# First norm of a streaming encoder step: rows turned and scaled in one product with a diagonal matrix of the roots, instead of scaled in place and then transposed

## What is computed

```
def _rmsnorm(x, g):
    y = xf * lax.rsqrt(jnp.mean(xf * xf, axis=-1, keepdims=True) + EPS)
    return y * g
...
h = _rmsnorm(x, g_mix[l])
qa, ka, va, qb, kb, vb, rb, a1, ga, gb = split(h @ w_in)
```

## Time and profile before

| what | value |
|---|---|
| median of three runs | 950.14 us |
| the profiled execution | 951.9 us |
| its span | 950.2 us |
| TensorE matmul busy | 897.2 us, 94% |
| VectorE busy | 577.5 us, 61% |
| ScalarE busy | 421.0 us, 44% |
| GpSimd busy | 273.9 us, 29% |

### The profile page before, as it was taken

The page is one execution under the profiler, slowest core; times in us unless marked ns, Lnnn a source line. Parts: engine busy times, 40 slices in busy tenths (PEclk is TensorE's granted clock), DMA queues, the critical chain, the costliest instruction groups (busy, mean ns, idle before and its releaser), DMA issues.

```text
span 950.2 us, 17215 instructions
## 1 busy us (share of the span) xinstructions
PE 897.2 (94%) x7051; PEld 855.9 (90%) x7051; DVE 577.5 (61%) x1115; ACT 421.0 (44%) x751; POOL 273.9 (29%) x161
## 2 busy tenths in 40 slices
PE   3999999999889999999999968899999999999997
PEld 3889999989888889888999958899999999999997
DVE  5582656557784445565545667785259884278842
ACT  5552443534453544445444445563235662155432
POOL 2442313222323223232333102225322225222351
PEclk9999999999998999999999979999999999999999
DMA  8323122121421221212114427774357774277522
GB/s 239 89 72 85 57 77 68 56 73 50 110 67 52 61 68 46 67 46 68 46 35 141 109 64 164 165 164 123 111 107 172 175 169 133 58 166 156 138 72 64
DMA packets 154293, 94.59 MB, mean 100 GB/s; under 512 B 4064, under 2 KB 145078, under 8 KB 154214
## 3 DMA queue, kind: packets, MB, share of 16 engines
q1 hardware_dynamic: 138246, 71.88, 26.9%
q0 software_dynamic: 9504, 17.31, 10.6%
q10 hardware_dynamic: 6464, 4.29, 1.7%
HBM read 71.87 MB, written 3.60 MB: 79 GB/s over the span
## 4 chain that ended last, share of the span: by engine, by line
PE 68%; DVE 15%; ACT 6%; DMA 6%; issue 3%; ACTq 1%; SPq 0%; POOL 0%; DVEq 0%; POOLq 0%
PE G L583 13%; PE G L585 12%; PE G L584 12%; PE X L845 3%; PE X L847 3%; PE X L848 3%; PE G L845 3%; PE G L847 3%; PE G L848 3%; DMA wraw<-in_w_up_dram 3%; PE X L752 2%; DVE qAT L1542 2%; DMA csum<-csum 2%; PE X L736 2%; PE X L723 1%
## 5 line engine op out<-in xcount | busy, mean ns | idle before, releaser
L583 PE MATMUL G<-h_hi,w_hi 128*128 128x272 f32 x1296 | 389.2, 300 | 6.7 <-DVE rv L1505 2.8
L585 PE MATMUL G<-h_hi,w_lo 128*128 128x272 f32 x1296 | 375.9, 290 | 0.0
L584 PE MATMUL G<-h_lo,w_hi 128*128 128x272 f32 x1296 | 374.6, 289 | 0.0
L532 POOL TENSOR_TENSOR w_lo<-wraw,w_hi 128x1024 fp32r<-128x1024 f32 x85 | 215.7, 2541 | 423.9 <-ACT w_hi L946 423.9
L583 PEld LDWEIGHTS G<-h_hi,w_hi 128*128 128x128 f32 x1296 | 245.3, 189 | 18.4 <-issue 13.8
L584 PEld LDWEIGHTS G<-h_lo,w_hi 128*128 128x128 f32 x1296 | 245.7, 190 | 0.6
L585 PEld LDWEIGHTS G<-h_hi,w_lo 128*128 128x128 f32 x1296 | 245.2, 189 | 0.0
L946 ACT ACTIVATE w_hi<-wraw 128x1024 fp32r<-128x1024 f32 x129 | 135.1, 1050 | 64.3 <-PE G L585 38.6
L1840 DVE TENSOR_TENSOR rs<-G,rv 128x544 f32<-128x544 f32 x24 | 17.4, 724 | 79.5 <-PE G L585 79.5
L1146 ACT ACTIVATE prob<-prob,nm 128x256 f32<-128x256 f32 (+2 forms) x80 | 36.7, 460 | 63.0 <-DVE sd L1574 63.0
L540 POOL DMA_DIRECT2D wraw<-csum x22 | 18.8, 857 | 158.6 <-DVE csum L1721 102.0
(11 more groups left out here) (299 smaller groups left out, 1826.4 us busy)
## 6 DMA issues: line engine op xcount, KB each, us to landing
wraw<-in_w_in_dram SPq DMA_DIRECT2D x53, 512.0 KB
wraw<-in_w_gate_dram SPq DMA_DIRECT2D x22, 512.0 KB
wraw<-in_w_up_dram SPq DMA_DIRECT2D x22, 512.0 KB
csum<-csum POOLq DMA_DIRECT2D x44, 256.0 KB, 6.2
wraw<-in_w_down_dram SPq DMA_DIRECT2D x16, 512.0 KB
wraw<-csum POOLq DMA_DIRECT2D x22, 256.0 KB, 3.5
wraw<-in_w_out_dram SPq DMA_DIRECT2D x8, 512.0 KB
wraw<-in_w_down_dram SPq DMA_DIRECT2D x8, 384.0 KB
```

The lines of the kernel that those rows point to most:

```text
L532: pool.tensor_tensor(w_lo[:, slot, :, :], wraw[:, slot, :, :], w_hi[:, slot, :, :].bitcast(F32), ALU.subtract).then_inc(w_split, 1)
L583: pe.matmul(o, w_hi[:, slot, kc, :], b_hi[:, kc, cols], start=(kc == 0), stop=False)
L584: pe.matmul(o, w_hi[:, slot, kc, :], b_lo[:, kc, cols], start=False, stop=False)
L585: mm = pe.matmul(o, w_lo[:, slot, kc, :], b_hi[:, kc, cols], start=False, stop=(kc == last))
```

## The change

The in-place scaling on ScalarE and VectorE goes. VectorE writes five diagonal matrices `root_diag` (in the memory of `att`) with the roots of the frames on the diagonal, and the turn of a row block is an ordinary float32 product of the block with its diagonal matrix, in place of a transposition with the identity.

```
-SCALE_ACT, SCALE_DVE = (0, 2), (1, 3, 4)
...
+        root_diag = att
...
             def turn_input(c):
-                if c % (KC // 2) == 0:
-                    pe.wait_ge(x_scaled_act, len(SCALE_ACT) * (1 + c // (KC // 2)))
-                    pe.wait_ge(x_scaled_dve, len(SCALE_DVE) * (1 + c // (KC // 2)))
                 if c >= 3:
                     pe.wait_ge(h_ok, c - 2)
                 for j, (t0, nt) in enumerate(TOK):
-                    mm = pe.transpose(TURNED[c % 3][:, t0:t0 + nt], xtok[0:nt, j, c * P:(c + 1) * P],
-                                      ident[0:nt, 0:nt])
+                    if c == 0:
+                        pe.wait_ge(diag_ok, j + 1)
+                    mm = pe.matmul(TURNED[c % 3][:, t0:t0 + nt], xtok[0:nt, j, c * P:(c + 1) * P],
+                                   root_diag[0:nt, j, 0:nt], start=True, stop=True)
                 mm.then_inc(x_turned, 1)
...
             high_part(0)
-            act.wait_ge(x_root, 1)
-            for part in range(2):
-                for j in SCALE_ACT:
-                    x = xtok[0:TOK[j][1], j, part * D // 2:(part + 1) * D // 2]
-                    act.activation(x, x, ACT.Copy, scale=rt[0:TOK[j][1], j:j + 1])\
-                        .then_inc(x_scaled_act, 1)
             act.wait_ge(param_ok, 1)
...
             refine(rv[:, 0:NJ], rt[:, 0:NJ], rs[:, 0:NJ], x_root)
+            dve.wait_ge(x_root, 1)
+            dve.wait_ge(const_pool, 1)
+            for j, (t0, nt) in enumerate(TOK):
+                dve.tensor_scalar(root_diag[0:nt, j, 0:nt], ident[0:nt, 0:nt], rt[0:nt, j:j + 1], None, ALU.mult)\
+                    .then_inc(diag_ok, 1)
             dve.wait_ge(setup_pe, 1)
             dve.tensor_copy(param[:, :], G[0][:, 0:24]).then_inc(param_ok, 1)
-            dve.wait_ge(x_root, 1)
-            for part in range(2):
-                for j in SCALE_DVE:
-                    x = xtok[0:TOK[j][1], j, part * D // 2:(part + 1) * D // 2]
-                    dve.tensor_scalar(x, x, rt[0:TOK[j][1], j:j + 1], None, ALU.mult).then_inc(x_scaled_dve, 1)
-
             dve.wait_ge(param_ok, 1)
```

More of the change, by code:

```diff
@@ L344, in mixer_program @@
         x_root = sem("x_root")
-        x_scaled_act = sem("x_scaled_act")
-        x_scaled_dve = sem("x_scaled_dve")
+        diag_ok = sem("diag_ok")
         x_turned = sem("x_turned")
```

## The result

The changed kernel takes 960.31 us (median of 4 runs, 957.77 to 960.95) against 949.55 before. The ratio is 1.0098, 95% interval [1.0063, 1.0132]: slower by 6 to 13 us, about 1%. The profiled execution took 960.69 us, its span 958.9.

What follows compares the result with a forecast made beforehand. TensorE, busy 94% of the span, was taken as the bound. An earlier start against slower turns summed to −0.3 to +0.4 us, put as no change, 950.2 us; range 947.1 to 954.2.

Steps and rivals of the forecast that it cites:

- What costs nothing: Work beside the turns: ScalarE, parameter copy and scalings, w_lo, DMA and VectorE were claimed to add no time.
- the 3.5 that I had named as a sign of being wrong: Weight tile 0: the prediction is wrong if chunk 7 starts more than 3.5 us away from 31.15.
- something unpriced further on: Later stretches of slow clock and of waits could fall otherwise; chance 0.05, split evenly between slower and faster.
- The product's price: Turns: a float32 product takes two passes, five passes more per turn, 0.55 us fast or 1.10 slow.
- The rival with four passes: Turns: a product costs four times a transposition's 0.11 us, giving +8.6 us, 958.8 us; chance 0.03.
- The fifth diagonal held: At the start, the sample tile's diagonal waits behind GpSimd's w_lo until 15.33 us, stalling turn 0.
- case B: At the start, the fifth diagonal is held until 15.33; turn 7 ends at 29.8 us, +0.4 us.
- The clock: TensorE at the start: rise to 2.4 GHz 5.2 us after the first ordinary product, near 17.5 us.
- late clock and case B: Start: clock rises at 24.5 and the fifth diagonal is held, +3.5 us, 953.7; late clock's chance 0.25.
- A shift is handed on one to one: Behind the first product TensorE has no gap, so a shift at 31 us reaches the total about one to one.
- The middle of A and B as forecast: Midpoint of fifth diagonal unheld (−0.3 us) and held (+0.4 us): no change, 950.2 us.
- the earlier start: TensorE's first turn starts at 12.33 instead of 15.45 us, 3.12 us earlier, since diagonals replace the scaling.

Runs made afterwards that it cites:

- e9: Kernel before, with 39 small idle transpositions (78 TensorE instructions) added at the start: 954.20 us, ratio 1.0054.
- e8: Kernel before, with GpSimd's first w_lo waiting for VectorE's six scalings: 946.37 us, ratio 0.9960.
- e12: Kernel before, with GpSimd's wait for the scalings and 39 small idle transpositions (78 instructions): 951.52 us, ratio 1.0017.
- e1: The changed kernel run again, unedited: 959.16 us against 949.06 for the kernel before, ratio 1.0102.
- e7: The changed kernel with 88 small idle transpositions added at the start, 254 instructions more than the kernel before: 954.24 us, ratio 1.0039 to that kernel.
- e2: The changed kernel with GpSimd's first w_lo waiting for the five diagonals: 957.32 us, ratio 1.0087 to the kernel before.
- e11: The changed kernel with GpSimd waiting for the diagonals and 89 small idle transpositions, 256 instructions more than the kernel before: 949.76 us, ratio 1.0001.
- e3: The changed kernel with turns as identity transpositions, diagonals still made, scaling left out of the computation: 948.92 us, ratio 0.9995 to the kernel before.
- e6: Kernel before, with GpSimd waiting for the scalings and making w_lo of weight tile 0 three times; TensorE's program untouched: 953.00 us, ratio 1.0035.
- e10: Kernel before, with 128 small idle transpositions (256 TensorE instructions) added at the start: 948.59 us, ratio 1.0003.

## Why the prediction was wrong

The step that failed is "What costs nothing", with its sentence that no DMA is moved or added: it put the stretch behind the start at nothing. TensorE's own program is fetched by DMA, and the change makes it 78 instructions longer at the front; that moved its blocks onto other weight loads 550 us later, and loads that a block falls on took up to 9.7 us instead of 5.9 to 6.8. It cost 4.7 us alone (e9) and 5.4 us on e8's version (e12), and 5.6 and 8.1 us came back where it was taken away (e1 to e7, e2 to e11). In five traces with 78 more the stretch is 362.4 to 365.9 us, in two with 50 more 362.3 and 364.0, in seven with −2, 0, 254 or 256 it is 356.8 to 360.9. The start missed too: chunk 7 came 3.7 us late, beyond the 3.5 that I had named as a sign of being wrong, by the clock and the held diagonals below. I had put 0.05 on "something unpriced further on" and hadn't looked for it.

- **The product's price** was right. Eighty records, two passes: turn at the fast level 26.65 − 25.20 = 1.45 us (forecast 1.36), at the slow level 2.57 us for the ten records of e11's third turn (2.39). The rival with four passes is out, although its 958.8 us lay near the result: a number that fits shows no mechanism.
- **The fifth diagonal held** (case B) was right in kind and too small. In the first profile, e1, e3 and e7 the row of five takes 3.11 to 3.15 us, since GpSimd started 0.2 to 0.7 us behind the first diagonal. In e1 it is the fifth that waits; in the first profile, e3 and e7 it is already the second. Which diagonal is caught changes with the landing of the rows and of weight tile 0.
- **The clock** was the other miss at the start. I took 5.2 us from the first ordinary product, from two places. The granted clock's first entry in the trace, where the spacing falls, stands 4.3 us (e2), 8.2 (first profile), 9.0 (e11), 11.4 (e1) and 14.0 us (e7) after it. With transpositions ahead it is 5.2 us in two traces (before and e3) and 2.4 to 9.5 us in the other seven. So there is no fixed distance, and two equal ones were chance. Nor did products in the turns bring the rise forward: it stands at 16.5 to 27.4 us in the five traces with the changed start, at 21.2 to 31.5 in the nine with transpositions. The rival (late clock and case B, +3.5 us) is what e1 did: rise at 23.8, fifth diagonal held, +3.7. The first profile's +3.7 is made up otherwise: the rise came at 21.5, but the second diagonal was held and the root was 1.0 us later.
- **A shift is handed on one to one** was about right: e6's 4.5 us in the trace came out as 3.2 in the total, and the 3.7 us of chunk 7 are 3.75 at 585 us in the changed kernel's first profile, but 2.2 in e1's.
- **The middle of A and B as forecast**, no change, holds only with both side costs gone, since the earlier start never had more than 3.1 us to give, against 8 turns' second pass. In e11, which has neither cost, the total is just even (1.0001), which is what the sum had said, though in its trace chunk 7 is 2.3 us late.

The 10.1 us of e1 split into some 5 to 8 for the place of the program and the rest, 2 to 5, for the start (3.7 in the traces); in the start the second pass and the late clock can't be told apart with these runs, since each execution has its clock somewhere else.

## What to carry to other kernels

A stretch that waits for loads can answer to a change in quite another place: compare the chain of waits there too, and pad an engine's program back to the old place (here a multiple of 256 instructions, in its idle time) before a loss or gain of a few microseconds is put down to the edit. Before one engine's work is rebuilt to start sooner, look for the single row that is several times longer than its twins: here a GpSimd operation held VectorE, and one wait gave what the new scheme didn't. A constant read from two places in one trace is worth a range, not a value.

## What the runs showed that was not expected

- The place of TensorE's program in steps of 256 instructions was worth 4.7 us of 950, with no change in any work but idle transpositions (e9 against before, 1.0054 [1.0036, 1.0073]; e10 1.0003). An up-weight load took 6.4 to 6.8 us in seven traces where no block's fetch fell on it and 8.4 to 9.3 in seven where one did.
- The rise to the 2.4 GHz level came 4.3 to 14.0 us after the first product of the same changed start.
- GpSimd held even a VectorE scaling of two columns: 2.21 us against 0.17 (L1375 in e2, L1373 in the first profile of the changed kernel).
